# Where the windowed attention's masks are added: from VectorE in PSUM to TensorE in the accumulation of the scores

## The chip, the cores and the metric

The program runs on one core of one Trainium2 chip. The metric is the device time of one execution, in microseconds (us); a kernel's time is the median of its runs.

## The reference

Two transformer blocks run one after the other on 512 tokens of width 1024, the first with 256 context tokens beside them. The first block's first layer has two attentions: one windowed with a sink (this case), then one with low-rank queries and keys. The windowed one, cut to what matters:

```python
WINDOW = 128            # SWA_HEADS 8, SWA_KV_HEADS 2, HEAD_DIM 64
valid = ((jnp.abs(qpos[:, :, None] - kpos[:, None, :]) <= WINDOW)
         & (kpos[:, None, :] >= 0) & (kpos[:, None, :] < S))
s_band = jnp.einsum('bnqhgd,bnkhd->bnhgqk', qb, kb).astype(jnp.float32) * scale
s_band = jnp.where(valid[None, :, None, None], s_band, NEG_INF)
s_ctx = jnp.einsum('bnqhgd,bchd->bnhgqc', qb, k_ctx).astype(jnp.float32) * scale
p = jax.nn.softmax(jnp.concatenate([s_ctx, s_band, sink_col], -1), axis=-1)
```

The context's own queries attend to the 256 context keys and the sink alone, without a mask.

## The kernel before

Every engine has its own program, written out by hand, and the engines meet only at semaphores. Nothing is reordered by a planner: an engine's order of work is the order of the lines in its block.

The windowed attention ("swa") is 24 units: four head pairs `p`, and for each six query tiles `i` of 128 rows. Tiles 0 to 3 are the 512 latent rows, tiles 4 and 5 the context rows. `key_tiles` (L481) lists a unit's key tiles of 128 columns: always the two context tiles, then for `i` below 4 the tiles `i - 1`, `i` and `i + 1` that exist. Tile `i - 1` carries the mask "before" and tile `i + 1` the mask "after", each a constant 128x128 matrix of 0 and -1e30. So per head pair, units 0 and 3 have four key tiles and one mask, units 1 and 2 five key tiles and two masks, units 4 and 5 two key tiles and no mask. In what follows the units are numbered 0 to 23 through the stage: pair 0 has 0 to 5, pair 1 has 6 to 11, and so on.

Each unit has two score tiles, `t` = 0 and 1, one for each head of the pair. Head 0 lies in partitions 0 to 63 of the query and key tensors, head 1 in partitions 64 to 127. Each has a PSUM slot of its own of 1024 columns, two banks (slots 0 and 1). The scores are matmuls of 64 rows by up to 256 columns; `score_runs` (L509) joins neighbouring key tiles. All of this is float32.

The order on TensorE in `pair_attention` (L694), for step `n`: the scores of unit `n` (both `t`); the transposes of the probabilities of unit `n - 1` (slot 2, spreading over slot 3); in 8 of the 24 steps one or two "modulation" columns, which are unrelated matmuls with 1 or 2 output columns, done in slot 4; and the values product of unit `n - 2`, in slot 4 too. Two units share one output in slot 4, so slot 4 has to be emptied before the next output or modulation.

The order on VectorE in `pair_attention` (L1843), for step `n`: for `t` = 0 and then 1, wait until the scores are filled, copy the sink into the column behind them (L1863), add the mask in PSUM (L1868 for both masks in one instruction of 256 columns, L1871 for one), wait for that to be done (`link`), and take the row maximum (L1874). Then the finished output of unit `n - 3` is taken out of slot 4, if it is odd (L1849, L1850), then the modulation columns (L1735), and then for each `t` the reciprocal of the sum (L1884) and the scaling of the probabilities (L1886). ScalarE takes the exponential of each score tile after its maximum (L1324), which empties the slot, and copies the transposes out (L1333).

The matmuls of every stage are recorded at one line, L549 (`mm`), the transposes of this stage at L717. A float32 matmul shows as two records, a transpose as one.

Of the kernel before, what the change touches and what calls it, by code (L numbers as in the profile page):

```python
# [20 lines left out]
ALU = mybir.AluOpType  # L21
# [3 lines left out]
P = 128  # L25
# [152 lines left out]
def build(nc, io, known):  # L178
# [4 lines left out]
    with ExitStack() as ctx:  # L183
# [124 lines left out]
        def slot(key):  # L308
            return known.get(("job", key), (0, 1))[0]

        def turn(key):
            return known.get(("job", key), (0, 1))[1]
# [188 lines left out]
            else:  # L501
                eng.wait_ge(outputs_done, value("outputs_done", u))

        def masked_tiles(u):

            masks = [(c, m) for c, (j, m) in enumerate(key_tiles(u)) if m]
            return [c for c, _ in masks], [m for _, m in masks]

        def score_runs(u):  # L509

            runs = []
# [35 lines left out]
        def _(pe):  # L547
            def mm(out, lhsT, rhs, first, last):
                return pe.matmul(out, lhsT, rhs, start=first, stop=last)  # L549
# [144 lines left out]
            def pair_attention(units, score, values, also):  # L694

                def scores(u, n):
                    for t in range(2):
                        key = (u, "scores", t)
                        take(key, t)
                        if turn(key) > 1:  # L700
                            pe.wait_ge(psum_drained[slot(key)], turn(key) - 1)
                        for c, j, nj in score_runs(u):
                            q, k = score(u, t, j, nj)
                            ins = mm(PS[slot(key)][:, c * P:(c + nj) * P], q, k, True, True)
                        ins.then_inc(psum_filled[slot(key)], 1)

                def transposes(u, n):
                    key = (u, "turned")
                    take(key, 2)
                    if turn(key) > 1:  # L710
                        pe.wait_ge(psum_drained[slot(key)], turn(key) - 1)
                    nk = len(key_tiles(u))
                    for t in range(2):
                        pe.wait_ge(rows_normalised, value("rows_normalised", (u, t)))
                        rows = pair_rows(u, n, t)
                        for c in range(nk):
                            ins = pe.transpose(PAIR_T[:, (nk * t + c) * P:(nk * t + c + 1) * P],  # L717
                                               rows[:, c * P:(c + 1) * P], const("ident"))
                    ins.then_inc(psum_filled[slot(key)], 1)

                def output(u, n):
                    key = out_job(u)
                    if u[2] % 2 == 0:
                        take(key, 4)
                        if turn(key) > 1:
                            pe.wait_ge(psum_drained[slot(key)], turn(key) - 1)
                    pe.wait_ge(psum_drained[slot((u, "turned"))], turn((u, "turned")))
                    at = P * (u[2] % 2)
                    tiles = key_tiles(u)
                    for c, (j, _) in enumerate(tiles):  # L730
                        for t in range(2):
                            k = (len(tiles) * t + c) * P
                            ins = mm(PS[slot(key)][HD * t:HD * t + HD, at:at + P], values(u, t, j),
                                     pair_turned(u, n)[:, k:k + P], c == 0, c == len(tiles) - 1)
                    if u[2] % 2:
                        ins.then_inc(psum_filled[slot(key)], 1)
                    else:
                        ins.then_inc(outputs_done, one("outputs_done", u))

                pe.wait_ge(psum_drained[3], given["slot", 3])  # L740
                for n in range(len(units) + 2):
                    if n < len(units):
                        scores(units[n], n)
                    if 1 <= n <= len(units):
                        transposes(units[n - 1], n - 1)
                    if n < len(units):
                        also(n)
                    if n >= 2:
                        output(units[n - 2], n - 2)
# [973 lines left out]
        def _(dve):  # L1723
# [119 lines left out]
            def pair_attention(units, first_tile, also):  # L1843
# [9 lines left out]
                for n in range(len(units) + 3):  # L1853
                    if n < len(units):
                        u = units[n]
                        w = len(key_tiles(u)) * P
                        at = 8 * (n % 2)
                        for t in range(2):
                            key = (u, "scores", t)
                            dve.wait_ge(psum_filled[slot(key)], turn(key))  # L1860
                            ps, k = PS[slot(key)], w
                            if u[0] == "swa":
                                ins = dve.tensor_copy(ps[:, w:w + 1], par("sink", 2 * u[1] + t, 1))  # L1863
                                at_c, masks = masked_tiles(u)
                                if len(masks) == 2:
                                    near = ps[:, 2 * P:6 * P].rearrange("p (b x c) -> p b x c", b=2, x=2)[:, :, 0, :]
                                    a, _ = C_AT["before"]
                                    ins = tt(near, near, C[:, a:a + 2 * P].rearrange("p (b c) -> p b c", b=2), ALU.add)  # L1868
                                elif masks:
                                    near = ps[:, at_c[0] * P:at_c[0] * P + P]  # L1870
                                    ins = tt(near, near, const(masks[0]), ALU.add)  # L1871
                                link(ins)
                                k += 1
                            dve.tensor_reduce(stat[:, at + t:at + t + 1], ps[:, 0:k], AX_X, ALU.max, negate=True)\  # L1874
                                .then_inc(row_max, one("row_max", (u, t)))
                    if n >= 3 and units[n - 3][2] % 2:
                        keep_output(units[n - 3])
                    if n < len(units):
                        also(n)
                        w = len(key_tiles(u)) * P  # L1880
                        for t in range(2):
                            dve.wait_ge(psum_drained[slot((u, "scores", t))], turn((u, "scores", t)))
                            inv = stat[:, at + 4 + t:at + 5 + t]
                            link(dve.reciprocal(inv, stat[:, at + 2 + t:at + 3 + t]))  # L1884
                            rows = pair_rows(u, n, t)[:, 0:w]
                            ts(rows, rows, inv, None, ALU.mult)\  # L1886
                                .then_inc(rows_normalised, one("rows_normalised", (u, t)))
# [702 lines left out]
```

## Time and profile before

| what | before |
|---|---|
| median of 3 runs (lowest, highest) | 3292.54 us (3290.94, 3295.78) |
| the profiled execution's own time | 3293.4 us |
| its span, first to last instruction | 3291.6 us |
| busy share of TensorE, its weight loads, VectorE, ScalarE, GpSimd | 91%, 73%, 51%, 29%, 21% |
| mean granted TensorE clock | 0.945 |
| windowed attention | from 197 to 350 us |

A share is over the whole span, while the change touches one stage of some 153 us. So the table says which engine is busiest in general, and the rows of that stage have to say what waits for what there. Busy matmul time is summed as a cover of the timeline; matmuls overlap, so their mean durations are longer than the distance between them.

### The profile page before, as it was taken

Reading aid. Unit: us, or ns where it says so; the run is one execution under the profiler, and the core shown is the slowest. Engines: PE = TensorE matmul, PEld = TensorE weight load, DVE = VectorE, ACT = ScalarE, POOL = GpSimd, SP = SyncE. Lnnn points to the kernel's source line nnn. Section 1 sums busy time; section 2 is a strip of 40 time slices with the busy share of each in tenths; the row PEclk is TensorE's granted clock in tenths of the full one; section 3 lists DMA queues with packets and bytes.
Section 4 is the critical chain, followed back from the end, with each engine's and each line's share of the span. In section 5 each row is a group of like instructions: output and inputs, shape, how many; then the busy total and the mean of one; then the engine's idle time right before and its main releaser. Section 6 shows DMA issues by size and latency. Waiting matters only on the chain.

```text
span 3291.6 us, 37169 instructions
## 1 busy us (share of the span) xinstructions
PE 3010.3 (91%) x14948; PEld 2391.0 (73%) x14948; DVE 1672.5 (51%) x2719; ACT 952.7 (29%) x1437; POOL 684.1 (21%) x752
## 2 busy tenths in 40 slices
PE   6988999899999998999889999777797899999999
PEld 5876467688888886776667888544475678778887
DVE  5255463443334327337645554489976643343333
ACT  1223352322112214135423233311024422232222
POOL 1535361074665402000001000054510000000000
PEclk9988999899999999999999999988877999999999
DMA  5211112022343221110013232111120023222232
GB/s 208 77 65 49 39 33 64 20 96 109 105 139 109 96 77 49 54 52 1 1 51 94 89 119 82 53 58 39 44 82 26 1 77 96 90 77 93 97 98 83
DMA packets 67338, 238.13 MB, mean 72 GB/s; under 512 B 7392, under 2 KB 10592, under 8 KB 66400
## 3 DMA queue, kind: packets, MB, share of 16 engines
q1 hardware_dynamic: 66880, 234.19, 21.8%
q8 instruction: 119, 1.95, 0.2%
q10 hardware_dynamic: 288, 1.57, 0.1%
q14 instruction: 51, 0.42, 0.0%
HBM read 233.64 MB, written 2.10 MB: 72 GB/s over the span
## 4 chain that ended last, share of the span: by engine, by line
PE 77%; DVE 15%; issue 3%; ACT 3%; POOL 2%; DMA 0%; ACTq 0%; DVEq 0%; SPq 0%; POOLq 0%
PE PSA L549 75%; ACT Y L1350 1%; DVE WS L1747 1%; DVE Y L1915 1%; DVE stat L1874 1%; DVE stat L1897 1%; DVE Y L2248 1%; PE PSA L717 1%; PE PSA L1189 1%; DVE Y L2245 1%; DVE Y L1914 1%; DVE Y L2244 1%; POOL X L1649 1%; DVE Y L1818 1%; DVE HS L1767 0%
## 5 line engine op out<-in xcount | busy, mean ns | idle before, releaser
L549 PE MATMUL PSA<-HS,WS 128*128 128x512 f32 (+1 forms) x7104 | 1492.2, 372 | 79.0 <-DVE HS L1767 44.3
L549 PEld LDWEIGHTS PSA<-HS,WS 128*128 128x128 f32 x7104 | 1241.9, 192 | 332.7 <-issue 90.6
L1747 DVE TENSOR_TENSOR WS<-W,WS 128x1024 fp32r<-128x1024 f32 (+2 forms) x358 | 421.4, 1178 | 609.5 <-ACT WS L1265 608.7
L1265 ACT ACTIVATE WS<-W 128x1024 fp32r<-128x1024 f32 (+2 forms) x358 | 351.1, 983 | 920.8 <-PE PSA L549 801.1
L549 PE MATMUL PSA<-YS,WS 128*128 128x512 f32 (+1 forms) x2688 | 561.6, 370 | 3.5 <-DVE YS L2368 3.5
L549 PEld LDWEIGHTS PSA<-YS,WS 128*128 128x128 f32 x2688 | 470.4, 189 | 91.2 <-DVE YS L2368 3.9
L549 PE MATMUL PSA<-Y 128*64 128x128 f32 (+8 forms) x2240 | 408.6, 387 | 95.3 <-DVE Y L2258 46.2
L549 PEld LDWEIGHTS PSA<-Y 128*64 128x64 f32 (+4 forms) x2240 | 252.6, 181 | 220.3 <-issue 95.4
L1669 POOL TENSOR_TENSOR MPROD<-W,silu_c 128x512 f32<-128x512 f32 x176 | 189.8, 1079 | 257.1 <-DMA W<-in_weights 244.3
L1649 POOL TENSOR_SCALAR X<-X 128x768 f32<-128x768 f32 (+1 forms) x32 | 65.3, 2069 | 640.1 <-DVE HS L1767 640.0
L1670 POOL TENSOR_TENSOR MPROD<-MPROD 128x256 f32<-128x256 f32 x176 | 154.4, 877 | 13.8
L1248 ACT ACTIVATE Y<-PSA 128x768 f32<-128x768 f32 (+3 forms) x85 | 61.0, 718 | 326.1 <-PE PSA L549 322.6
L1937 DVE SCALAR_TENSOR_TENSOR Y<-PSA,PR,Y 128x511 f32<-128x511 f32 x66 | 41.6, 658 | 183.1 <-ACT Y L1375 183.0
L1713 POOL TENSOR_TENSOR Y<-Y 128x512 f32<-128x512 f32 x16 | 19.7, 1230 | 525.7 <-ACT Y L1248 409.8
L549 PE MATMUL PSA<-Y,C 128*128 128x512 f32 (+2 forms) x220 | 101.6, 595 | 22.9 <-ACT Y L1580 7.8
L1955 DVE TENSOR_TENSOR Y<-Y,PSA 128x512 f32<-128x512 f32 (+1 forms) x66 | 51.2, 776 | 133.9 <-PE PSA L549 133.6
L1324 ACT ACTIVATE Y<-PSA,stat 128x768 f32<-128x768 f32 (+4 forms) x96 | 67.8, 706 | 151.7 <-DVE stat L1874 140.5
L1798 DVE SCALAR_TENSOR_TENSOR X<-PSA,MOD,X 128x512 f32<-128x512 f32 x72 | 45.4, 659 | 123.6 <-PE PSA L549 123.6
L1375 ACT ACTIVATE Y<-PSA,PR 128x768 f32<-128x768 f32 (+1 forms) x44 | 39.0, 886 | 228.0 <-PE PSA L549 228.0
L549 PE MATMUL PSA<-WS,HS 128*128 128x512 f32 (+2 forms) x528 | 97.9, 349 | 2.0 <-DVE Y L1777 2.0
L549 PEld LDWEIGHTS PSA<-WS,HS 128*128 128x128 f32 x528 | 84.9, 194 | 15.8 <-issue 4.3
L1927 DVE TENSOR_TENSOR YS<-Y,YS 128x512 fp32r<-128x512 f32 (+1 forms) x66 | 52.9, 801 | 81.1 <-ACT YS L1365 81.1
(254 smaller groups left out, 2643.7 us busy)
## 6 DMA issues: line engine op xcount, KB each, us to landing
W<-in_weights SPq DMA_DIRECT2D x396, 512.0 KB, 3.5
Y<-in_early SPq DMA_DIRECT2D x4, 2048.0 KB, 14.5
W<-in_weights SPq DMA_DIRECT2D x24, 256.0 KB, 2.6
X<-in_x SPq DMA_DIRECT2D x1, 3072.0 KB, 28.4
W<-in_weights SPq DMA_DIRECT2D x24, 128.0 KB, 2.1
Y<-in_ssm ACTq DMA_DIRECT2D x1, 1024.0 KB, 7.0
out<-X SPq DMA_DIRECT2D x1, 1024.0 KB, 4.6
C<-in_consts SPq DMA_DIRECT2D x1, 948.5 KB, 33.9
```

The source lines that it names most:

```text
L549: return pe.matmul(out, lhsT, rhs, start=first, stop=last)
L1248: act.activation(dst, ps[rows, lo:lo + n], func, scale=scale).then_inc(psum_drained[slot(key)], 1)
L1265: act.activation(WS[:, n % R_RING, 0, 0:f], W[:, c % W_RING, 0:f], ACT.Copy)\
L1324: act.activation(pair_rows(u, n, t)[:, 0:w], PS[slot(key)][:, 0:w], ACT.Exp, bias=stat[:, at + t:at + t + 1], accum_out=stat[:, at + 2 + t ...
L1649: ins = pool.tensor_scalar(X[:, k, 0:n], X[:, k, 0:n], ALPHA, None, ALU.mult)
L1669: link(pool.tensor_tensor(MPROD[:], w[:, 4 * h:4 * h + 4, :], c, ALU.mult))
L1670: link(pool.tensor_tensor(MPROD[:, 0:2], MPROD[:, 0:2], MPROD[:, 2:4], ALU.add))
L1747: tt(WS[:, n % R_RING, 1, 0:f], W[:, c % W_RING, 0:f], WS[:, n % R_RING, 0, 0:f].bitcast(F32), ALU.subtract).then_inc(weights_split, 1)
L1798: ins = stt(X[:, m, lo:lo + n], ps[:, lo:lo + n], gate(m, s), X[:, m, lo:lo + n], ALU.mult, ALU.add)
L1927: tt(a[:, 1, m - ms[0], :], GC[:, m % 3, 0:n], a[:, 0, m - ms[0], :].bitcast(F32), ALU.subtract).then_inc(activated, one("activated", (f, m)))
L1937: ins = stt(gc[:, lo + 1:lo + nn], ps[:, lo:lo + nn - 1], par("conv_w", f * 66 + m, 1), gc[:, lo + 1:lo + nn], ALU.mult, ALU.add)
L1955: tt(gc[:, 0:n], gc[:, 0:n], ps[:, 0:n], ALU.mult).then_inc(psum_drained[slot(("up", f, m))], 1)
```

## The change

VectorE's mask addition is gone. TensorE adds the masks itself: after all score matmuls of a score tile it issues, for each masked key tile, one matmul of the identity (stationary, 128x128) with the mask (moving, 128x128) into the same PSUM columns, without the flag that starts a new sum. The semaphore that tells VectorE that the scores are filled moves to the last of these. The sink column is still copied by VectorE, and the wait (`link`) after it stays.

```diff
@@ helper removed
-        def masked_tiles(u):
-
-            masks = [(c, m) for c, (j, m) in enumerate(key_tiles(u)) if m]
-            return [c for c, _ in masks], [m for _, m in masks]
@@ TensorE, pair_attention, scores
+                        masks = [(c, m) for c, (j, m) in enumerate(key_tiles(u)) if m]
                         for c, j, nj in score_runs(u):
                             q, k = score(u, t, j, nj)
-                            ins = mm(PS[slot(key)][:, c * P:(c + nj) * P], q, k, True, True)
+                            near = any(c <= a < c + nj for a, _ in masks)
+                            ins = mm(PS[slot(key)][:, c * P:(c + nj) * P], q, k, True, not near)
+                        for c, name in masks:
+                            ins = mm(PS[slot(key)][:, c * P:(c + 1) * P], const("ident"), const(name), False, True)
                         ins.then_inc(psum_filled[slot(key)], 1)
@@ VectorE, pair_attention
                                 ins = dve.tensor_copy(ps[:, w:w + 1], par("sink", 2 * u[1] + t, 1))
-                                at_c, masks = masked_tiles(u)
-                                if len(masks) == 2:
-                                    near = ps[:, 2 * P:6 * P].rearrange("p (b x c) -> p b x c", b=2, x=2)[:, :, 0, :]
-                                    a, _ = C_AT["before"]
-                                    ins = tt(near, near, C[:, a:a + 2 * P].rearrange("p (b c) -> p b c", b=2), ALU.add)
-                                elif masks:
-                                    near = ps[:, at_c[0] * P:at_c[0] * P + P]
-                                    ins = tt(near, near, const(masks[0]), ALU.add)
                                 link(ins)
```

## Rows read from the trace of the kernel before

**Rows 1.** The page, part 2: granted TensorE clock in 40 slices of the span.

```profile
PEclk9988999899999999999999999988877999999999
```

**Rows 2.** The chain that ended last, shares by line, 197 to 350 us.

```profile
by line: PE PSA L549 52.0%; DVE stat L1874 14.1%; PE PSA L717 6.5%; issue 5.5%; DVE Y L1886 4.3%; DVE HS L1850 3.4%; DVE HS L1849 2.8%; DVE PSA L1863 2.4%; DVE MOD L1735 2.3%; DVE PSA L1868 2.2%; ACT Y L1324 2.0%; DVE PSA L1871 1.8%; DVE st
```

**Rows 3.** Waits, 195 to 350 us: total, times, longest, in us.

```profile
DVE PSA L1863 <- PE PSA L549: 27.1, 16, 2.7
...
PEld PSA L549 <- issue: 25.7, 47, 3.3
PE PSA L549 <- DVE HS L1850: 17.4, 12, 2.4
```

**Rows 4.** Groups by shape, 195 to 350 us: count, busy us, mean ns.

```profile
L1868 DVE TENSOR_TENSOR PSA<-PSA,C 128x256 f32<-128x256 f32 x16 | 6.8, 423 | 0.0
...
L1871 DVE TENSOR_TENSOR PSA<-PSA,C 128x128 f32<-128x128 f32 x16 | 4.6, 289 | 0.0
```

**Rows 5.** Timeline of VectorE, units 6 to 8: start us, length us.

```profile
237.87 0.16 DVE L1863 COPY PSA<-PR 128x1 f32<-128x1 f32 x1
...
238.26 0.69 DVE L1874 TENSOR_REDUCE stat<-PSA 128x1 f32<-128x513 f32 x1
...
239.26 0.69 DVE L1874 TENSOR_REDUCE stat<-PSA 128x1 f32<-128x513 f32 x1
...
242.77 0.16 DVE L1863 COPY PSA<-PR 128x1 f32<-128x1 f32 x1 [0.84 <-PE PSA L549]
...
243.29 0.82 DVE L1874 TENSOR_REDUCE stat<-PSA 128x1 f32<-128x641 f32 x1
...
248.78 0.82 DVE L1874 TENSOR_REDUCE stat<-PSA 128x1 f32<-128x641 f32 x1
```

**Rows 6.** Timeline of the weight loads, units 6 to 8, clock at 1.0.

```profile
236.71 0.74 PEld L549 LDWEIGHTS PSA<-Y 64*128 64x128 f32 x8 [0.17 <-issue]
237.78 0.42 PEld L717 LDWEIGHTS PSA<-C,Y 128*128 128x128 f32 x4 [0.33 <-issue]
...
241.38 1.70 PEld L549 LDWEIGHTS PSA<-Y 64*128 64x128 f32 x12 [0.17 <-issue]
243.20 0.86 PEld L717 LDWEIGHTS PSA<-C,Y 128*128 128x128 f32 x8
...
245.09 2.42 PEld L549 LDWEIGHTS PSA<-Y 64*128 64x128 f32 x12 [0.45 <-ACT Y L1324]
247.62 1.07 PEld L717 LDWEIGHTS PSA<-C,Y 128*128 128x128 f32 x10
```

**Rows 7.** Windows over the stationary-128, moving-128 float32 matmuls of tile stat.

```profile
1632.30:1635.20 2.90, 2.83 (x13) 0.50 0.00 0
1636.00:1640.40 4.40, 4.40 (x42) 1.00 0.00 0
```

**Rows 8.** Timeline of TensorE's matmuls, units 1 and 8.

```profile
201.78 3.52 PE L549 MATMUL PSA<-Y 64*128 64x256 f32 x12 [2.01 <-ACT Y L1324]
...
245.09 2.61 PE L549 MATMUL PSA<-Y 64*128 64x256 f32 x12 [0.21 <-ACT Y L1324]
```

**Rows 9.** Timeline of the weight loads, unit 22.

```profile
337.28 0.29 PEld L549 LDWEIGHTS PSA<-Y 64*128 64x128 f32 x2 [0.17 <-issue]
337.74 0.29 PEld L549 LDWEIGHTS PSA<-Y 64*128 64x128 f32 x2 [0.16 <-ACT Y L1324]
```

**Rows 10.** Timeline of VectorE, unit 22.

```profile
338.32 0.15 DVE L1863 COPY PSA<-PR 128x1 f32<-128x1 f32 x1
```

**Rows 11.** Timeline of the weight loads, unit 1, clock at 0.5.

```profile
201.78 3.22 PEld L549 LDWEIGHTS PSA<-Y 64*128 64x128 f32 x12 [2.73 <-ACT Y L1324]
205.22 1.57 PEld L717 LDWEIGHTS PSA<-C,Y 128*128 128x128 f32 x8 [0.22 <-issue]
```

**Rows 12.** Windows, the ten stretches at clock 0.5, TensorE: length, busy (x), clock.

```profile
195.00:212.10 17.10, 12.68 (x49) 0.50 0.17 62
...
253.00:259.90 6.90, 6.59 (x38) 0.51 0.24 76
...
sum 71.80, PE 64.53; mean PE 6.45
```

## The prediction

> **What bounds the kernel now.** I read the page's slices first: the granted clock is near full nearly everywhere and dips to 8 tenths in slices 3 and 4, which is where the windowed attention lies [rows 1]. The rest of the kernel is untouched, so next came the chain of waits cut to 197 to 350 us. There the work alternates: TensorE's matmuls and transposes hold 52.0% + 6.5%, VectorE's row maximum 14.1%, and the two mask lines 2.2% + 1.8% [rows 2]. So neither engine bounds the stage alone; they hand the work to each other. The waits say the same from both sides: VectorE waited 27.1 us for scores at the sink copy, TensorE 17.4 us for the emptied output slot [rows 3]. Behind the stage TensorE goes straight on with the projections of the second attention, and it is the chain there too, so I take what the stage gains or loses as gained or lost at the end, one for one.
>
> **What is removed.** 32 VectorE instructions, 6.8 + 4.6 = 11.4 us busy [rows 4]. Of these the chain holds 4.0% of 153 us = 6.1 us [rows 2]; the others lie beside TensorE's work and cost nothing now. One of 256 columns delays its row maximum by 0.34 us (it overlaps the sink copy), one of 128 by 0.21 us: the copy starts at 242.77 and the maximum at 243.29, against 237.87 and 238.26, each with 0.16 of copy and about 0.02 of wait besides [rows 5]. So 6.1 us is the most that the change can give by itself.
>
> **What is added.** Six masks for each head pair and score tile, so 48 matmuls, two records each: 96. The nearest rows are matmuls of just this shape with a constant operand, later in the kernel: 13 records in 2.83 us at clock 0.5 (0.218) and 42 in 4.40 us at 1.0 (0.105, with one or two counted that began before) [rows 7]. I take 0.11 at the full level (1.0, 2.4 GHz) and 0.215 at the half level (0.5, 1.2 GHz). A mask then costs 0.22 or 0.43 us, the 96 records 10.6 or 20.6 us of TensorE, all of it in front of the semaphore on which VectorE waits.
>
> **What is lost beside it.** The trace shows a second cost that the diff doesn't name. The two score tiles use different halves of the rows, and their loads run side by side. In unit 6 the eight passes of both tiles take 237.78 - 236.71 = 1.07 us up to the transposes. In unit 7 the twelve passes take 243.20 - 241.38 = 1.82 us; in unit 8, whose second tile came late because its slot was still being read, 247.62 - 245.09 = 2.53 us [rows 6]. That is the price of running them in series: 0.7 us for a unit with two masks. A tile there is 1.27 alone; without its two short passes (0.11 each) it is 1.05, so a unit with one mask loses 1.0 us. After the change a full-height matmul stands between the two tiles in program order, and I expect the second tile not to pass it. No row shows such a sequence, so the bounds are 0 (it passes) and the 0.7 and 1.0 us. I take the upper ones: in the rows the transposes, also full height, never start before the last score load.
>
> Then the changes of shape. Each first load of another shape follows a gap of 0.17 us [rows 6], 0.22 at half level [rows 11]. Before there is one between scores and transposes; afterwards three (into a mask, out of it, into the second) and none before the transposes. Two more: 0.34 us, bounds 0 and 0.68, as the gap may be hidden or the first pass be slow too.
>
> Together, TensorE's program for a unit grows by:
> - two masks: 4 x 0.22 + 0.7 + 0.34 = 1.9 us
> - one mask: 2 x 0.22 + 1.0 + 0.34 = 1.8 us
> - at half level, with 0.43 for a mask and the other terms about doubled, some 3.5 us for either
>
> A rule of the Trainium skill bears on that choice (TensorE: Matmul & The Clock Gate, Part 3, The mechanism): a weight load overlaps a running matmul only where it goes to other row groups, and matmuls start and end in program order. By it a full-height mask can have no second tile beside it, which is the sum taken here; without it the first rival's sum would hold. Units 6 to 8 agree with the rule in what they do show, 1.07 and 1.82 us against 2.53; no row has a full-height matmul in between.
>
> **How much of it lies on the path.** I walk one head pair, units 6 to 11, at full level.
>
> Unit 6 (one mask), bound by VectorE. TensorE starts the scores at 236.71; with 1.07 + 1.8 the second tile is filled at 239.58. Copy and maximum take 0.16 + 0.02 + 0.69, so the second maximum ends at 240.5 instead of 239.95: +0.55. VectorE was free before that; the two additions that went (0.42) are inside this number. The output slot is emptied behind it, and unit 7's scores wait for that.
>
> Units 7 and 8 (two masks each). Unit 7's scores start at 241.38 + 0.55 = 241.93. From there to unit 8's scores TensorE needed 245.09 - 241.38 = 3.71, of which it idled 0.21 [rows 8]; now 3.50 + 1.9, so unit 8 starts at 247.3. Its two tiles in series with masks take 2.53 + 0.88 + 0.34 = 3.75: filled at 251.05, maximum done at 251.05 + 1.0 = 252.1. Before it was 248.78 + 0.82 = 249.60: +2.5 for the three units together. TensorE has taken over as the bound here. What comes next (output slot emptied, modulation columns, output of unit 6) is late by as much.
>
> Unit 9 (one mask), unit 10. TensorE is the path: outputs, scores, transposes, outputs, scores. In unit 22, the like place of the last pair, the scores of unmasked tiles start at 337.28 [rows 9], and VectorE takes them at 338.32, held up by its own work [rows 10]. With +1.8 they start at 339.1 and are there at about 339.5: +1.2. Units 10 and 11 have no mask. A pair: 2.5 + 1.2 = 3.7; three pairs 11.1 us.
>
> In pair 1 unit 9 falls in the stretch 253.0 to 259.9, at half level [rows 12], and the cover isn't there: 3.5 instead of 1.2, so +2.3.
>
> Pair 0 begins at half level. Unit 0: 3.5 less the 2.0 us that TensorE idled before unit 1 [rows 8] = 1.5; units 1 and 2: 3.5 each. That is 8.5 by 212.1, but what slides past the end of this stretch runs at double speed, so 4.3 remain; unit 3 adds 1.2: 5.5.
>
> Sum: 11.1 + 2.3 + 5.5 = 18.9 us. Against it stands the same sliding at the nine later stretches, 54.7 us together (71.8 less 17.1) [rows 12]. It can't be worked out, since the stretches may move with the work; between 0 and, by the measure of the first, half of the delay. I take 5.9 off, leaving +13. The profiled execution was at 3293.4 us, its span 3291.6, 0.9 us above the median of the runs; against the median the forecast is 3292.5 + 13 = 3305.5 us.
>
> **The rivals.**
>
> The second tile does stream beside the masks. Then only the first tile's fill is late, 8 x (0.22 + 0.17) + 8 x (0.44 + 0.17) = 8.0 us, the rest hidden behind the first row maximum, and the 6.1 us come off: +2, 3294.5 us. For it: the two halves do run side by side today. Against it: the transposes never do with scores. No difference that a measurement shows.
>
> The clock turns it into a gain. TensorE is at half level for 71.8 us here with 64.5 us busy [rows 12]; half of that, 32 us, is what full level would give back. Fewer idle stretches (the 17.4 us waiting for the output slot shrink) and 96 more full-height passes could raise the level sooner. It decides from the point where 13 + 6.6 = 20 us come back, six tenths of these stretches. If two thirds of them go: 3305.5 - 21 = 3284.5. For it: there are ten such stretches in the stage, so the level is near its edge. Against it: the stretches follow the modulation columns, which stay; and the first 17.1 us are at half level with TensorE 74% busy. The Trainium skill says, on the same page under Why this matters for your kernels, to avoid gaps in order to keep the full clock; by that rule fewer waits would mean this rival, and no row here settles it.
>
> It costs nearly all of its price everywhere: 8 x 1.8 + 8 x 1.9 = 29.6 us less the 6.1 = 23.5, 3316 us. For it: half-level stretches, where VectorE's cover is too short. Against it: the walk above.
>
> **How the numbers follow.** Forecast case 0.75 (3299.5 to 3311), the overlap kept 0.13, the clock 0.05, the full price 0.07. The range reaches down to the overlap rival's 3294.5 and up to 3314, near the full price: 3294 to 3314. About 0.2%, 6.6 us, is what a measurement of this kernel can tell from no change. Slower by more than that: 0.75 and 0.07, less the forecast case's lower edge: 0.80. Within: 0.15. Faster: 0.05.
>
> **What the profile of the changed kernel would show.** L1868 and L1871 are gone. 96 matmul records of shape 128x128 with both operands from the constants, 0.11 us apart at full level, with a gap before and behind. In masked units the second tile's first load comes only behind the first tile's masks, and the weight loads of units 6 and 7 take about 3 us and 3.7 us up to the transposes. VectorE waits longer at the sink copy: 27.1 us grow by some 15 or more. TensorE's wait for the output slot, 17.4 us, shrinks. The stage ends 13 us later and everything behind it has its old length. The prediction is wrong if the second tile's loads start before the masks are through, if a change of shape costs nothing, or if the half-level stretches in the stage become much shorter than 71.8 us.

## The result and the profile after

| | median us | runs from | to |
|---|---|---|---|
| before | 3294.16 | 3290.94 | 3298.60 |
| after | 3329.36 | 3324.27 | 3332.97 |

Four runs each. The ratio is 1.0105, with an interval of 1.0086 to 1.0123: slower by 35 us. The forecast was 3305.5, its range ended at 3314. The sign was right, the size was wrong by almost a factor of three.

The profiled execution of the changed kernel took 3328.94 us, its span is 3327.1. In the page's slices the granted clock is lower early in the span than in [rows 1]:

```profile
PEclk9976999999999999999999999888877899999999
```

From here on "the stage" is the windowed attention, from its first score matmul to its last output kept. Before it lasts from 197.70 to 349.70 us, 152.0. These windows of the changed kernel show length, busy time of TensorE, weight loads, VectorE, ScalarE and GpSimd, granted clock, DMA share and GB/s. The first row is the stage, the second its longest stretch at half level, the third the second attention, whose code is untouched.

```profile
201.70:386.20 184.50, 167.09 (x960) 131.16 (x960) 79.66 (x232) 56.32 (x120) 68.35 (x96) 0.73 0.13 41
298.70:332.90 34.20, 33.48 (x135) 27.20 (x136) 11.17 (x29) 8.36 (x15) 10.05 (x14) 0.50 0.10 31
434.00:559.00 125.00, 115.32 (x826) 83.15 (x826) 82.87 (x168) 64.51 (x117) 72.87 (x96) 0.93 0.12 37
```

The stage grew by 32.5 us and holds nearly the whole loss. It starts 4.0 us later: from 160 us to its start the mean clock was 0.89, against 0.96 before, under the same code. The second attention is 7.5 us longer than before (125.0 against 117.5), with a part at half level where before it had none. The rest of the kernel gives about 8 back: the changed kernel is 36.5 us late at the end of the stage and 35.5 at the end of the span. The longer second attention is also in the traces of kernels that are as fast as the one before (the seventh and the tenth below), and it is missing in the trace of the second kernel below, whose TensorE program is the changed kernel's: 117.5 us again. So it is scatter of the clock and not the change's.

The chain of waits in the stage, by line (L544 is the matmul helper, L549 before; L716 the transposes; L1865 the row maximum):

```profile
by line: PE PSA L544 74.1%; PE PSA L716 10.9%; DVE stat L1865 4.1%; DVE HS L1849 2.6%; issue 2.2%; DVE HS L1848 2.1%; DVE MOD L1734 1.9%; DVE PSA L1862 1.1%; DVE Y L1877 0.4%; DVE Y L1778 0.4%; ACT Y L1323 0.3%; DVE stat L1875 0.2%
```

Against [rows 2] TensorE's share went from 58.5% to 85.0% and the row maximum fell from 14.1% to 4.1%. The waits, total, times and longest in us, beside those of [rows 3]:

```profile
DVE PSA L1862 <- PE PSA L544: 74.1, 40, 3.6
...
PEld PSA L544 <- issue: 36.3, 83, 3.2
...
PE PSA L544 <- DVE HS L1849: 11.6, 11, 1.3
```

VectorE's wait for scores grew from 27.1 to 74.1 us, TensorE's wait for the output slot shrank from 17.4 to 11.6. The two engines no longer take turns at being late; TensorE is late nearly always.

The weight loads of unit 6, at full level, answer to [rows 6]. One record of a load or a matmul is called a pass here; a float32 matmul has two:

```profile
247.74 0.73 PEld L544 LDWEIGHTS PSA<-Y 64*128 64x128 f32 x4 [0.18 <-issue]
248.80 0.30 PEld L544 LDWEIGHTS PSA<-C 128*128 128x128 f32 x2 [0.33 <-issue]
249.21 0.73 PEld L544 LDWEIGHTS PSA<-Y 64*128 64x128 f32 x4
250.27 0.30 PEld L544 LDWEIGHTS PSA<-C 128*128 128x128 f32 x2 [0.33 <-issue]
250.49 0.47 PEld L716 LDWEIGHTS PSA<-C,Y 128*128 128x128 f32 x4
```

They read like the forecast: scores of one tile, its mask, scores of the other tile, its mask, and the second tile's loads start only behind the first tile's mask. From the scores to the transposes 2.75 us went by, against 1.07 before: +1.68, forecast +1.8. Unit 8 has two masks for each tile. It too ran at full level, and reached the transposes 3.64 us after its first score load; the walk had 3.75:

```profile
261.57 1.16 PEld L544 LDWEIGHTS PSA<-Y 64*128 64x128 f32 x6 [0.17 <-issue]
262.85 0.52 PEld L544 LDWEIGHTS PSA<-C 128*128 128x128 f32 x4
263.49 1.16 PEld L544 LDWEIGHTS PSA<-Y 64*128 64x128 f32 x6
264.77 0.52 PEld L544 LDWEIGHTS PSA<-C 128*128 128x128 f32 x4
265.21 0.91 PEld L716 LDWEIGHTS PSA<-C,Y 128*128 128x128 f32 x8
```

At half level the forecast had some 3.5 us more for either kind of unit. Unit 14, with two masks, took 314.48 - 307.67 = 6.81 us:

```profile
307.67 2.21 PEld L544 LDWEIGHTS PSA<-Y 64*128 64x128 f32 x6 [0.33 <-issue]
...
313.68 0.93 PEld L544 LDWEIGHTS PSA<-C 128*128 128x128 f32 x4 [0.23 <-issue]
314.48 0.66 PEld L716 LDWEIGHTS PSA<-C,Y 128*128 128x128 f32 x3
```

Unit 1 before took 205.22 - 201.78 = 3.44 us at half level [rows 11], so that is 3.4 us more.

So the prices of a unit were right and their sum was not. Where it went is seen by head pair. These are windows from the first row maximum of one pair to that of the next, before:

```profile
200.22:238.26 38.04, 33.40 (x204) 27.60 (x204) 22.07 (x62) 13.41 (x29) 19.98 (x28) 0.66 0.18 53
238.26:275.36 37.10, 30.47 (x222) 24.53 (x220) 21.56 (x67) 13.90 (x30) 19.73 (x28) 0.82 0.16 49
275.36:313.46 38.10, 30.78 (x222) 24.88 (x220) 23.57 (x67) 13.90 (x30) 20.34 (x29) 0.82 0.19 60
313.46:349.70 36.24, 28.71 (x214) 22.49 (x212) 23.40 (x68) 14.60 (x31) 8.28 (x12) 0.81 0.09 30
```

and after:

```profile
204.80:249.52 44.72, 42.19 (x225) 33.26 (x225) 18.11 (x55) 13.53 (x29) 19.83 (x28) 0.67 0.13 38
249.52:294.61 45.09, 40.32 (x245) 31.53 (x244) 20.07 (x58) 14.03 (x30) 18.77 (x28) 0.77 0.13 45
294.61:346.32 51.71, 47.85 (x245) 38.06 (x244) 20.39 (x58) 14.14 (x30) 19.94 (x29) 0.64 0.13 39
346.32:386.20 39.88, 33.66 (x242) 26.28 (x240) 20.93 (x61) 14.63 (x31) 9.81 (x14) 0.87 0.12 37
```

Time at half level in a window is 2 x (1 - clock) x length, since the clock is at one of two levels.

| pair | forecast us | measured us | half level before | after |
|---|---|---|---|---|
| 0 | 5.5 | 6.7 | 26 | 30 |
| 1 | 3.7 + 2.3 | 8.0 | 13 | 21 |
| 2 | 3.7 | 13.6 | 14 | 37 |
| 3 | 3.7 | 3.6 | 14 | 10 |

Pair 2 is the one in which the stretch of 34.2 us lies, and it is out by 10 us. The four sum to 31.9 against 18.9 in the forecast; the 5.9 us that the forecast took off aren't there either. At half level the same work takes about twice as long (6.81 us for unit 14, 3.64 for unit 8), so where TensorE bounds, half of the added time at half level is time lost. Less that half, the pairs lost 4.7, 4.0, 2.1 and 5.6 us, 16.4 together, against 3.7 each at full level in the walk. So the last pair's 3.6 is near the walk partly by luck: it spent some 4 us less at half level than before.

### The profile page after: what moved, and what is told of

Read it like the earlier page. It is cut to its first block, busy times and chain, and to the rows that moved or that the text cites. A ratio compares the mean times of both kernels' runs of the same rounds, so it can differ in the third digit from the quotient of the medians.

```text
span 3327.1 us, 37329 instructions
## 1 busy us (share of the span) xinstructions
PE 3068.6 (92%) x15044; PEld 2427.7 (73%) x15044; DVE 1663.5 (50%) x2687; ACT 953.6 (29%) x1437; POOL 688.3 (21%) x752
## 4 chain that ended last, share of the span: by engine, by line
PE 79%; DVE 13%; ACT 3%; issue 3%; POOL 1%; DMA 0%; ACTq 0%; DVEq 0%; SPq 0%; POOLq 0%
PE PSA L544 77%; PE PSA L716 1%; ACT Y L1349 1%; DVE WS L1746 1%; DVE Y L1906 1%; DVE stat L1888 1%; DVE Y L2239 1%; PE PSA L1188 1%; DVE Y L1905 1%; DVE Y L2236 1%; DVE Y L2235 1%; POOL X L1648 1%; DVE Y L1817 1%; DVE stat L1865 0%; DVE HS L1766 0%
## 5 line engine op out<-in xcount | busy, mean ns | idle before, releaser
L544 PE MATMUL PSA<-HS,WS 128*128 128x512 f32 (+1 forms) x7104 | 1500.2, 373 | 78.8 <-DVE HS L1766 44.3
L544 PEld LDWEIGHTS PSA<-HS,WS 128*128 128x128 f32 x7104 | 1247.4, 192 | 339.0 <-issue 94.5
L544 PE MATMUL PSA<-YS,WS 128*128 128x512 f32 (+1 forms) x2688 | 561.6, 370 | 3.5 <-DVE YS L2359 3.5
L544 PEld LDWEIGHTS PSA<-YS,WS 128*128 128x128 f32 x2688 | 470.4, 189 | 91.3 <-DVE YS L2359 3.9
L544 PE MATMUL PSA<-Y 128*64 128x128 f32 (+8 forms) x2240 | 435.8, 392 | 82.1 <-DVE Y L2249 38.3
L544 PEld LDWEIGHTS PSA<-Y 128*64 128x64 f32 (+4 forms) x2240 | 267.9, 183 | 214.0 <-issue 100.5
L544 PE MATMUL PSA<-Y,C 128*128 128x512 f32 (+2 forms) x220 | 104.1, 608 | 22.9 <-ACT Y L1579 7.8
L1673 POOL TENSOR_TENSOR MSUM<-MPROD 128x128 f32<-128x128 f32 x88 | 43.9, 499 | 282.3 <-PE PSA L544 278.4
L544 PE MATMUL PSA<-WS,HS 128*128 128x512 f32 (+2 forms) x528 | 97.5, 347 | 2.0 <-DVE Y L1776 2.0
L544 PEld LDWEIGHTS PSA<-WS,HS 128*128 128x128 f32 x528 | 84.5, 193 | 15.9 <-issue 4.3
```

The costliest lines, as they stand in the source:

```text
L1673: link(pool.tensor_tensor(total, MPROD[:, 0], MPROD[:, 1], ALU.add))
```

## The experiments

The theory after the result: TensorE lost the overlap of the two tiles as forecast, and above that price the stage now stays longer at half level. The rivals: VectorE's side matters more than thought, or the masks themselves cost more. The other numbers in this section are the stage's windows and the medians; a ratio is always to the kernel before, run on the same chip in the same rounds.

### The removal alone, and the addition alone

The first kernel removes VectorE's mask additions and puts nothing in their place.

```diff
                                 ins = dve.tensor_copy(ps[:, w:w + 1], par("sink", 2 * u[1] + t, 1))
-                                at_c, masks = masked_tiles(u)
-                                if len(masks) == 2:
...
-                                    ins = tt(near, near, const(masks[0]), ALU.add)
                                 link(ins)
```

> Before without VectorE's mask additions and with nothing in their place, so the masks are left out of the scores. Removal alone. Theory A (the chain read before the change was right about VectorE's part): 6 us faster than before. Theory B (TensorE's clock level decides the stage, and VectorE's part is noise beside it): within 3 us of before, unless the low stretches change.

3296.01 us against 3296.24, ratio 0.9992 (0.9981 to 1.0003). The stage took 149.2 us instead of 152.0. Its time at half level, 75 us, is not less than before. The forecast's ceiling for this gain was 6.1 us, from the chain's 4.0%. What was measured lies between 6.3 us gained and 1.0 lost, so the ceiling isn't contradicted, and neither theory is excluded.

The second kernel is the changed one with VectorE's additions put back, so that each mask is added twice.

> The changed kernel with VectorE's additions put back as well, so each mask is added twice (-2e30 instead of -1e30). Addition alone. Theory A (TensorE's program is the path in nearly every masked unit after the change): within 3 us of the changed kernel. If VectorE were still the path in half of the units, some 5 us slower than it.

Its edit restores in the changed kernel the lines that the first one removes. 3333.84 us, ratio 1.0115 (1.0098 to 1.0131), beside 1.0105 for the change. VectorE does some 10 us of work more and the time is the same within the intervals: in the changed kernel VectorE's side of the stage lies beside TensorE's. TensorE's program is the same in the two, so this is a second trace of the changed kernel's stage. It shows the same mean clock and a stretch of the same length at half level:

```profile
197.30:383.50 186.20, 167.35 (x960) 130.77 (x960) 89.31 (x264) 56.07 (x120) 68.12 (x96) 0.73 0.13 40
290.20:324.40 34.20, 33.29 (x132) 26.82 (x132) 12.97 (x35) 7.78 (x15) 10.04 (x14) 0.50 0.11 31
```

### The order alone

The third kernel keeps the masks on VectorE and only makes TensorE finish the first score tile before it starts the second, in the masked units.

```diff
+                        if t and u[0] == "swa" and u[2] < 4:
+                            pe.wait_ge(psum_filled[0], turn((u, "scores", 0)))
                         for c, j, nj in score_runs(u):
```

> Before, masks on VectorE, but in masked units TensorE waits for the first score tile to be filled before it begins the second: the loss of the overlap by itself, with no mask matmul. Theory A: 8 x 1.0 + 8 x 0.7 = 13.6 us of TensorE plus 16 waits of some 0.2 us, about half on the path at full level: +8 us, up to +16 with low stretches. Theory B (the clock level falls because the two row halves no longer run together): the time at half level in the stage rises from 66 to near the changed kernel's 97 us, and the time by 15 us or more.

3326.03 us, ratio 1.0091 (1.0076 to 1.0107): 30 us, with no mask matmul at all. Its stage:

```profile
200.90:381.70 180.80, 161.56 (x864) 124.36 (x864) 90.52 (x264) 56.48 (x120) 67.94 (x96) 0.67 0.14 42
```

Two tiles in series with half-height passes cost nearly what the whole change costs, and the clock mean is still lower than after the change, 0.67: 119 us at half level against 70 before and 100 after. The matmuls don't come to more than before (864). This is what the second theory expected, the first had +16 us at most. The wait itself takes part: unit 6 took 2.31 us from its first score load to the transposes, 0.39 more than the like unit of the fifth kernel below, which has no wait.

The fourth kernel is the changed one with the order put right: the scores of both tiles first, then the masks of both.

```diff
+                        if not masks:
+                            ins.then_inc(psum_filled[slot(key)], 1)
+                    for t in range(2 if masks else 0):
+                        key = (u, "scores", t)
                         for c, name in masks:
                             ins = mm(PS[slot(key)][:, c * P:(c + 1) * P], const("ident"), const(name), False, True)
                         ins.then_inc(psum_filled[slot(key)], 1)
```

> The changed kernel with the order scores of both tiles, masks of both tiles: the same 96 mask records, but the two tiles' scores side by side again and one change of shape fewer. Theory A: the overlap's loss was 13.6 us at full and some 27 us at half level, so 13 to 25 us faster than the changed kernel, that is +10 to +20 against before. Theory B (the mask records themselves lower the clock level): under 8 us faster than the changed kernel, with over 90 us at half level in the stage.

3301.92 us, ratio 1.0020 (1.0009 to 1.0031). The weight loads of its unit 6:

```profile
237.12 0.74 PEld L544 LDWEIGHTS PSA<-Y 64*128 64x128 f32 x8 [0.17 <-issue]
238.19 0.52 PEld L544 LDWEIGHTS PSA<-C 128*128 128x128 f32 x4 [0.33 <-issue]
238.63 0.47 PEld L720 LDWEIGHTS PSA<-C,Y 128*128 128x128 f32 x4
```

Eight score passes in 1.07 us, as before the change, and 0.44 for the two masks: 1.51 us where the changed kernel has 2.75. The same 96 mask records, and of the 35 us some 6 are left. Both theories had more left: +10 to +20 us, or under 8 us gained on the changed kernel with over 90 us at half level. Its stage:

```profile
197.60:350.80 153.20, 130.32 (x960) 107.19 (x960) 81.37 (x232) 55.81 (x120) 68.80 (x96) 0.82 0.16 49
```

It was at half level for 55 us. So the 96 records by themselves don't bring the changed kernel's 100.

### The height of the passes

Serial passes cost TensorE time by themselves and went with more time at half level. To part the two, the fifth and sixth kernels start from the one before and have the same program order; they differ in the rows that the score matmuls of the masked units use. In the fifth both tiles use rows 0 to 63, so they can't run side by side; in the sixth both use all 128. The scores of both are others than the reference's.

```diff
-                r = slice(HD * t, HD * t + HD)
+                r = slice(HD * t, HD * t + HD) if i >= 4 else slice(0, HD)
```

The sixth has `slice(0, P)` at the end of this line.

> Before, masks on VectorE, but in masked units both score tiles use partitions 0 to 63, so they can't run side by side (both tiles hold the first head's scores, the second head's are left out). Serial without any added semaphore wait or mask matmul, half of the rows in use. Theory A (a longer TensorE program, priced at whatever level is granted) and theory B (one row half at a time keeps the granted clock at the half level) both expect near the serial run before it: +25 to +30 us, over 90 us at half level in the stage.

> The same, but both score tiles use all 128 partitions (each holds the sum of both heads' scores). Same length of TensorE's program and same serial order as the same-half run, twice the rows in use. Theory A: the same time as the same-half run, within 5 us. Theory B: the level is granted back, under 60 us at half level in the stage, and +8 to +14 us against before, so some 15 us faster than the same-half run.

The fifth: 3318.33 us against 3296.94, ratio 1.0075 (1.0058 to 1.0092). Its stage, and the stretch at its beginning:

```profile
200.30:371.10 170.80, 150.11 (x864) 121.26 (x864) 91.34 (x264) 56.32 (x120) 68.15 (x96) 0.70 0.13 42
196.20:233.70 37.50, 34.02 (x130) 26.35 (x129) 17.55 (x46) 10.41 (x20) 10.05 (x14) 0.50 0.18 56
```

The sixth: 3295.17 us, ratio 0.9990 (0.9978 to 1.0002), better than the +8 to +14 us of its expectation. Its stage:

```profile
197.70:348.30 150.60, 126.93 (x864) 104.72 (x864) 91.17 (x264) 55.77 (x120) 68.52 (x96) 0.82 0.15 49
```

Both have two tiles in series, 864 matmuls and no mask on TensorE. The one with half the rows is 20.2 us longer in the stage. Their programs are not quite of one length. From the first score load to the transposes a unit with two masks, at full level, took 2.37 us in the fifth kernel and 2.16 in the sixth:

```profile
257.85 2.25 PEld L549 LDWEIGHTS PSA<-Y 64*128 64x128 f32 x12 [0.17 <-issue]
260.22 1.08 PEld L717 LDWEIGHTS PSA<-C,Y 128*128 128x128 f32 x10
```

```profile
244.47 2.25 PEld L549 LDWEIGHTS PSA<-Y 128*128 128x128 f32 x12 [0.17 <-issue]
246.63 1.12 PEld L717 LDWEIGHTS PSA<-C,Y 128*128 128x128 f32 x10
```

The loads take the same 2.25 us; the fifth has a change of shape before the transposes and the sixth none. A unit with one mask took 1.92 us (from 245.86) and 1.61 (from 234.20). Over 16 units that is 4 us at full level, and more where the level is half. Half-level time is 102 us in the fifth and 54 in the sixth; half of the difference, 24 us, is more than the whole gap. So most of the fifth kernel's loss beside the sixth is clock. The sixth is as fast as the kernel before although its tiles are in series, but it also spent some 15 us less at half level than that one did; how much of the lost overlap VectorE hides and how much the clock paid back isn't separated by these two.

The seventh kernel makes the same edit to the changed kernel: its order, its 96 mask records, scores of full height.

> The changed kernel with full-height scores in the masked units (each tile holds the sum of both heads' scores): masks on TensorE, serial, no change of shape between scores and masks. Theory A: 16 x 3 changes of 0.1 to 0.17 us fewer, so some 5 to 8 us faster than the changed kernel. Theory B: +8 to +15 us against before, so 20 us or more faster than the changed kernel.

3298.90 us, ratio 1.0004 (0.9993 to 1.0015): 30 us faster than the changed kernel. Its stage, and its weight loads in unit 8 at full level:

```profile
200.20:353.10 152.90, 134.42 (x960) 114.00 (x960) 83.75 (x232) 55.78 (x120) 68.40 (x96) 0.84 0.16 49
```

```profile
242.78 1.16 PEld L544 LDWEIGHTS PSA<-Y 128*128 128x128 f32 x6 [0.17 <-issue]
243.86 0.53 PEld L544 LDWEIGHTS PSA<-C 128*128 128x128 f32 x4
244.31 1.17 PEld L544 LDWEIGHTS PSA<-Y 128*128 128x128 f32 x6
245.40 0.53 PEld L544 LDWEIGHTS PSA<-C 128*128 128x128 f32 x4
245.84 1.12 PEld L716 LDWEIGHTS PSA<-C,Y 128*128 128x128 f32 x10
```

The order is still serial, and the unit takes 3.06 us against 3.64 for the like unit of the changed kernel, because the gaps at the changes of shape are gone. That is 0.58 us, over 16 units 9 us at full level and somewhat more where the level is half, of the 31.6 between the two stages. At half level the one spent 100 us and the other 49, and half of that difference is 25 us: the larger part is clock. The expectation had +8 to +15 us against the kernel before and was too cautious.

The eighth is the fourth with identity and masks in bfloat16, so that a mask is one record and not two.

```diff
-                            ins = mm(PS[slot(key)][:, c * P:(c + 1) * P], const("ident"), const(name), False, True)
+                            ins = mm(PS[slot(key)][:, c * P:(c + 1) * P], MB[:, 0:P],
+                                     MB[:, P:2 * P] if name == "before" else MB[:, 2 * P:3 * P], False, True)
```

> The masks-last order with identity and masks in bfloat16 (two casts on ScalarE ahead of the stage): one record per mask instead of two, 48 instead of 96. If what is left of the masks-last run's loss is the mask records on TensorE's path (some 5 to 10 us of them), this takes half of it off: 2 to 5 us faster than that run, level with before or up to 2 us faster. If the loss is scatter of the clock stretches, no difference from it.

3297.62 us, ratio 1.0013 (1.0002 to 1.0023), beside 1.0020 for the fourth. The stage took 149.6 us with 48 records fewer. The two intervals overlap, so a gain over the fourth kernel isn't shown; against the kernel before it is none. Which of that expectation's two cases holds stays open.

### Full height with the reference's scores

The sixth and seventh kernels compute other scores. The next two get full height with the scores of the reference: a second copy of the keys, and in each copy the 64 rows of the other head are zero. The ninth is the kernel before with this edit, the tenth the changed kernel with it. VectorE writes copy and zeros, three instructions for each half of the keys.

```diff
-                r = slice(HD * t, HD * t + HD)
-                return QS[r, p, i * P:(i + 1) * P], KS[r, p // 2, j * P:(j + n) * P]
+                if i == 0 and t == 0 and p in (0, 2):
+                    pe.wait_ge(keys_split, value("keys_split", p // 2))
+                return QS[:, p, i * P:(i + 1) * P], (KS, KS1)[t][:, p // 2, j * P:(j + n) * P]
...
+            def split_keys(g):
+                up = slice(HD, P)
+                link(dve.tensor_copy(KS1[up, g, :], KS[up, g, :]))
+                dve.memset(KS1[0:HD, g, :], 0.0)
+                dve.memset(KS[up, g, :], 0.0).then_inc(keys_split, one("keys_split", g))
```

> Before, masks on VectorE, with full-height scores in all units that give the reference's result: VectorE copies each key head into a tile of its own and zeroes the other head's rows in both (6 instructions of some 0.5 to 0.9 us, half of them ahead of the stage, half beside it), so the stationary operand holds both query heads and the moving one has 64 rows of zeros. If what keeps the level up is the height of the instruction, near the full-height run: 0 to 3 us faster than before, some 50 us at half level in the stage. If rows of zeros don't count, near the same-half run: +20 us and 95 us or more at half level.

> The changed kernel with the same full-height scores on padded keys: masks on TensorE, no change of shape between scores and masks, the reference's result. If the height counts: within 3 us of the run after-with-full-height, level with before, 30 us faster than the changed kernel. If rows of zeros don't count: +25 us or more against before.

The ninth: 3297.26 us against 3294.77, ratio 1.0006 (0.9998 to 1.0015). The tenth: 3296.95 us, ratio 1.0004 (0.9995 to 1.0012). The stages of the ninth and the tenth:

```profile
200.50:354.30 153.80, 130.79 (x864) 109.89 (x864) 92.58 (x267) 55.78 (x120) 68.37 (x96) 0.81 0.16 49
197.60:348.90 151.30, 132.44 (x960) 113.72 (x960) 84.16 (x235) 55.82 (x120) 68.61 (x96) 0.87 0.16 50
```

The ninth was at half level for 58 us, near the sixth kernel's 54 and the some 50 of its expectation, but the 0 to 3 us of gain that this expected are not there. Its trace is of its slowest run, 3306.5 us. The tenth had 39 us, the least of all. So full height with rows of zeros has about the time of full height with rows of data, and none of the fifth kernel's loss. The tenth does what the change wants, with 96 mask records and two tiles in series, and its time can't be told from the kernel's before; it is some 32 us faster than the changed kernel. It doesn't beat the kernel before.

### More overlap

If serial half-height passes hold the clock down, passes that overlap better might raise it. The eleventh kernel is the one before with the score matmuls of the two tiles issued in turn.

```diff
+                        for c, j, nj in runs:
+                            for t in ts_:
+                                key = (u, "scores", t)
+                                q, k = score(u, t, j, nj)
+                                ins = mm(PS[slot(key)][:, c * P:(c + nj) * P], q, k, True, True)
```

> Before, masks on VectorE, with the score matmuls of the two tiles issued in turn instead of tile after tile, so both halves start together in units with two masks too (today the second starts 0.5 us late). If more overlap both shortens TensorE's program and raises the level: 2 to 6 us faster than before, under 60 us at half level in the stage. If waiting for both slots before the first matmul costs as much: no difference.

3305.71 us, ratio 1.0027 (1.0016 to 1.0039): 9 us slower. Its stage:

```profile
201.10:362.00 160.90, 125.18 (x864) 101.54 (x864) 92.36 (x264) 55.71 (x120) 67.91 (x96) 0.74 0.15 45
```

The expected gain did not come. The stage was at half level for 84 us against 70, which is 7 of the 8.9 us that the stage grew, at the same TensorE busy time as before. To take turns it has to wait for both score slots before its first score matmul, so it idles more; that this idling is the cause was not tried apart.

### Half level in all runs

So far a kernel's time at half level is that of one execution. The span and the mean granted clock are known for every run, so the same formula gives the half-level time of the whole program for all of them. Means over the runs, in us; "before" stands for the kernel before on the same chip (for the changed kernel, for all 68 runs of it on the three chips of the experiments):

| kernel | runs | half level | before | longer than before | half of the added half level | rest |
|---|---|---|---|---|---|---|
| changed | 4 | 406 | 371 | 34.5 | 17.5 | 17 |
| first, no masks | 10 | 377 | 371 | -2 | 3 | -5 |
| second, both additions | 4 | 410 | 371 | 37.5 | 19 | 18 |
| third, serial | 4 | 419 | 371 | 30 | 24 | 6 |
| fourth, masks last | 10 | 374 | 371 | 7 | 2 | 5 |
| fifth, same half | 4 | 406 | 372 | 21 | 17 | 4 |
| sixth, full height | 10 | 357 | 372 | -3 | -7 | 4 |
| seventh, changed at full height | 10 | 349 | 372 | 1 | -11 | 12 |
| eighth, masks in bfloat16 | 10 | 382 | 372 | 2 | 5 | -3 |
| ninth, padded keys | 11 | 375 | 369 | 3 | 3 | 0 |
| tenth, padded keys and masks | 11 | 348 | 369 | 2 | -11 | 12 |
| eleventh, in turn | 7 | 386 | 369 | 9 | 8 | 1 |

The runs of one kernel scatter in it by 6 to 17 us (one standard deviation), which leaves some 2 to 6 us on a mean. The last two columns are an estimate, since half of the added time at half level is lost only where TensorE bounds. By it the clock is half of the changed kernel's loss and all but 4 to 6 us of the third's and the fifth's. The seventh and the tenth aren't free of cost: serial order and masks take some 12 us, and less time at half level pays 11 back. The ninth doesn't show the sixth kernel's lower half-level time, so whether rows of zeros raise the level as much as rows of data is open there, while the seventh and the tenth agree (349 and 348).

## Why the prediction was right in its parts and wrong in its sum

**The removal.** Called 6.1 us at most. The run without the additions showed 0.2, between a gain of 6.3 and a loss of 1.0; less the clock's part in all runs the estimate is a gain of 5. So the 6.1 is neither confirmed nor excluded.

**A mask's price.** 0.22 us at full level; the rows of unit 8 in the seventh kernel have 0.45 for two, the fourth kernel's unit 6 has 0.44. Right.

**The lost overlap and the changes of shape.** +1.8 and 3.75 us forecast, +1.68 and 3.64 found. Apart, the overlap was priced a little high and the changes of shape a little low. The fifth kernel's serial units are 0.85 us (1.92 less 1.07) and 0.55 us (2.37 less 1.82) longer than those before, forecast 1.0 and 0.7; what then is left for the changes of shape is 0.39 us a unit (2.75 - 1.92 - 0.44), forecast 0.34. The forecast's rule, that the second tile's loads don't pass the first tile's masks, is in the rows. The first rival, that they do, is excluded. The Trainium skill says that a weight load overlaps matmuls in flight only where its row group is another (TensorE: Matmul & The Clock Gate, Part 3, The mechanism). A full-height matmul leaves no other row group, and the runs agree: 2.75 us with the masks between the tiles, 1.51 with them behind both. It also says (TensorEngine Tiling (Array Packing), Key Properties) that a change of mode drains TensorE; it gives no price. Here the gaps cost 0.58 us a unit by the difference to full height, 3.64 less 3.06.

**The walk through the queue.** TensorE did take over as the bound. Without the clock's part the pairs lost 16.4 us together, and the rest of the changed kernel in all runs is 17, where the walk had 18.9 with some 4 us of it for half level (the 2.3 in pair 1 and 1.8 in pair 0). The sum was about right. The single pairs weren't all: 2.1 us in pair 2 and 5.6 in pair 3, forecast 3.7 each.

**The step that failed** is the clock's: "Against it stands the same sliding at the nine later stretches, 54.7 us together (71.8 less 17.1) [rows 12]. It can't be worked out, since the stretches may move with the work; between 0 and, by the measure of the first, half of the delay. I take 5.9 off". It took the half-level stretches as given, let work slide out of them, and bounded the term at zero from the wrong side. The time at half level wasn't given, it belonged to the new order: about 70 us before, 100 after, and 35 us more in the mean of all runs. Half of the 30 is 15 us lost, in place of 5.9 gained. With 18.9 for the walk the sum is 34, without the walk's 4 us for half level 30, and the stage grew by 32.5. The forecast's own sign of failure asked only for stretches that become much shorter; they became longer. The reading of [rows 1] that it began with was also short: slices 27 to 31 are at 8 and 7 tenths too. No term of the sum hangs on that.

**The rival of the clock** had the right thing in the wrong direction. It said that fewer waits and more passes could raise the level. TensorE's wait for the slot did shrink and its busy share rose to 91% of the stage (167.09 of 184.50), and the level fell. For 34.2 us it stayed at 0.50, the level of 1.2 GHz, with TensorE busy for 33.48. The Trainium skill's advice to keep TensorE busy without gaps in order to keep the full clock (TensorE: Matmul & The Clock Gate, Why this matters for your kernels) doesn't explain this stretch, in which hardly a gap was left to close.

**The rival of the full price**, 23.5 us, would have been nearer in size, for a reason that was not the one measured. By it every pair would have lost 5.9 us, at full level and with no more clock than before. Pairs 0, 1 and 3, less the clock's part, lost 4.7, 4.0 and 5.6, between the walk and this rival, and pair 2 lost 2.1. The four together, 16.4, speak for the walk and against 23.5, but not each pair does.

**Shown and not shown.** Shown: serial order without a mask costs 21 to 30 us (third and fifth kernels); the masks without serial order 6 (fourth); serial order and masks with full-height passes none on balance (seventh and tenth). Not shown: what in a half-height pass holds the level down. The fifth and the sixth kernels differ in the rows of the passes, but with the rows a change of shape in each masked unit goes too, and no run has one without the other, so this rival stands. The kernels before and with masks last have such changes as well, at 70 and 55 us of half level, so it isn't their presence alone. Not shown either: why in the eleventh kernel the level fell; and why the second attention was 7.5 us longer in some traces. Ahead of the stage and in the second attention the level also moved between kernels whose code there is equal, and the profile gives one execution of each, so a single stage's half-level time is uncertain by some 10 us (39 and 49 in two traces of nearly the same program, the tenth and the seventh); the ratios don't depend on it.

## What to carry to other kernels

Before a full-height matmul is put between matmuls of half height, look in the weight loads at whether the small ones run in pairs. If they do, put it behind both of them, or give the small ones full height with rows of zeros. Take the clock's level in a stage as part of what a change does to the order of the passes, not as its background, and bound that term on both sides: here 5.9 us gained was forecast and some 15 were lost, a difference larger than the whole forecast of 13.

## What was not expected of the hardware

- TensorE stayed at the half level for 34.2 us while busy for 33.48 of them, in a stretch that alternates serial half-height score passes with full-height ones; the second kernel did so for 34.2 us at 33.29 busy, the fifth for 37.5 us at 34.02.
- The same order with passes of 128 rows halved the time at half level, from 102 to 54 us without masks and from 100 to 49 with them; with 64 rows of zeros it came to 58 and 39. What in the height does it isn't shown.
- A float32 matmul at 128 rows took TensorE no longer than one at 64: six passes with their loads in 1.16 us in both the changed and the seventh kernel. The zeros cost nothing on TensorE, and full height saved the gaps at the changes of shape.
